# A memory stage with tokens on the partitions: numerators and denominators from one product, diagonals one item ahead

## What is computed

```python
def step(carry, inp):
    C, n, m = carry
    ...
    s = jnp.einsum('bthd,bshd->bhts', qc, kc) * jnp.exp(d - m_t[..., None])
    num = jnp.einsum('bhts,bshe->bhte', s, vc) + w_inter[..., None] * jnp.einsum('bthd,bhde->bhte', qc, C)
    den = s.sum(-1) + w_inter * jnp.einsum('bthd,bhd->bht', qc, n)
    h = num / jnp.maximum(jnp.abs(den), jnp.exp(-m_t))[..., None]
...
hn = hf * lax.rsqrt(jnp.mean(hf * hf, axis=-1, keepdims=True) + EPS)
hn = hn * g_ml.astype(jnp.float32).reshape(ML_HEADS, ML_V_DIM)
ml = hn.reshape(B, T, ML_WIDTH).astype(att.dtype) * jax.nn.sigmoid(o_pre)
```

## Time and profile before

| | us |
|---|---|
| time before, median of 3 runs | 2726.67 (2722.68 to 2727.57) |
| the profiled execution | 2733.2 |
| its span | 2731.4 |
| memory stage, layer 0: loop | 281.0 to 370.3 |
| first half of the output product, layer 0 | 370.3 to 389.3 |
| memory stage, layer 1: loop | 1030.8 to 1086.9 |
| first half of the output product, layer 1 | 1086.9 to 1096.6 |

### The profile page before, as it was taken

The page is one execution under the profiler, slowest core; times in us unless marked ns, Lnnn a source line. Parts: engine busy times, 40 slices in busy tenths (PEclk is TensorE's granted clock), DMA queues, the critical chain, the costliest instruction groups (busy, mean ns, idle before and its releaser), DMA issues.

```text
span 2731.4 us, 34159 instructions
## 1 busy us (share of the span) xinstructions
PE 2568.9 (94%) x13662; PEld 2099.3 (77%) x13662; DVE 1824.8 (67%) x2870; ACT 1310.2 (48%) x1937; POOL 29.5 (1%) x27
## 2 busy tenths in 40 slices
PE   6999998999999989799999999999989899998998
PEld 3464665778787658788888888887788899997998
DVE  4778433667532354399999989988867576576774
ACT  2135313222222243287777777776745454444543
POOL 0000000000000000000000000000000000000000
PEclk8999898999998998799999999999989999998999
DMA  6422001555421110298898888997933355432552
GB/s 280 186 101 100 1 31 62 192 207 185 160 102 62 47 47 1 93 356 328 334 357 328 332 339 329 349 334 301 366 133 111 125 182 191 151 139 100 178 182 97
DMA packets 71676, 512.08 MB, mean 187 GB/s; under 512 B 7904, under 2 KB 9056, under 8 KB 10048
## 3 DMA queue, kind: packets, MB, share of 16 engines
q1 hardware_dynamic: 68688, 500.20, 49.2%
q10 hardware_dynamic: 2208, 7.37, 0.7%
q0 software_dynamic: 592, 1.97, 0.2%
HBM read 507.27 MB, written 2.23 MB: 187 GB/s over the span
## 4 chain that ended last, share of the span: by engine, by line
PE 82%; DVE 9%; ACT 6%; issue 1%; DMA 1%; DVEq 0%; ACTq 0%
PE bank L767 81%; DVE UL L1906 2%; ACT UH L1456 1%; DVE arena L1906 1%; ACT arena L1459 1%; DVE arena L1914 1%; DVE HT L1906 1%; DMA XT<-in_x 1%; PE bank L1099 1%; ACT HT L1459 1%; DVE HGl L1906 1%; ACT XT L1459 0%; DVE arena L1910 0%; DVE JUNK L1953 0%; DVE small L1973 0%
## 5 line engine op out<-in xcount | busy, mean ns | idle before, releaser
L1906 DVE TENSOR_TENSOR UL<-ring,UH 128x1024 fp32r<-128x1024 f32 x738 | 886.1, 1212 | 216.1 <-ACT UH L1456 196.7
L1456 ACT CAST UH<-ring 128x1024 fp32r<-128x1024 f32 x738 | 761.2, 1039 | 353.6 <-PE bank L767 345.0
L767 PE MATMUL bank<-XH,UH 128*128 128x256 f32 x1040 | 308.2, 296 | 9.9 <-DVE XL L1906 8.8
L767 PE MATMUL bank<-UH,HGh 128*128 128x512 f32 (+1 forms) x768 | 293.1, 382 | 14.3 <-DVE HT L1906 10.3
L767 PE MATMUL bank<-XL,UH 128*128 128x256 f32 x1040 | 297.0, 286 | 0.0
L767 PE MATMUL bank<-XH,UL 128*128 128x256 f32 x1040 | 296.8, 285 | 0.0
L767 PE MATMUL bank<-UL,HGh 128*128 128x512 f32 (+1 forms) x768 | 289.1, 376 | 3.5 <-issue 3.5
L767 PE MATMUL bank<-UH,HGl 128*128 128x512 f32 (+1 forms) x768 | 289.7, 377 | 0.0
L1456 ACT CAST UH0a<-ring 128x1024 fp32r<-128x1024 f32 x66 | 69.0, 1048 | 319.9 <-PE bank L767 314.5
L767 PEld LDWEIGHTS bank<-XH,UH 128*128 128x128 f32 x1040 | 201.4, 194 | 22.4 <-issue 15.3
L1953 DVE CUSTOM_DVE_ANT_0 JUNK<-ring,CROW 128x1024 bf16<-128x1024 f32 x176 | 206.0, 1217 | 18.3 <-ACT CROW L1459 17.3
(11 more groups left out here) (206 smaller groups left out, 4513.5 us busy)
## 6 DMA issues: line engine op xcount, KB each, us to landing
ring<-in_w SPq DMA_DIRECT2D x477, 1024.0 KB, 4.8
XT<-in_x ACTq DMA_DIRECT2D x1, 2048.0 KB, 20.4
bias_scratch<-BIAS POOLq DMA_DIRECT2D x6, 192.0 KB, 2.1
consts<-in_c ACTq DMA_DIRECT2D x1, 1109.0 KB, 7.9
CROW<-in_r ACTq DMA_DIRECT2D x1, 1024.0 KB, 13.5
out_y<-XT ACTq DMA_DIRECT2D x2, 512.0 KB, 3.5
BIAS<-bias_scratch POOLq DMA_DIRECT2D x1, 768.0 KB, 5.7
constd<-in_c ACTq DMA_DIRECT2D x1, 768.0 KB, 4.1
```

The costliest lines, as they stand in the source:

```text
L767: return e.matmul(out, lhsT, rhs, start=start, stop=stop, skip_group_check=True)
L1456: return e.copy(out, in_)
L1906: return e.tensor_tensor(out, a, b, op)
```

## The change

`V_M` gets 129 columns a head, the last filled with ones by POOL (memories behind it move by 16 columns). The product of an item is turned: for each covered block of 128 target tokens the weighted scores are stationary and the 129 columns stream, so that a bank receives numerators with tokens on the partitions and, beside them, the denominators. A group takes two such banks in layer 0 (two blocks each), one in layer 1. The products with the column of ones, `feedback`, `divided`, `squares_of` and `norm_of` are gone. `denominator` reads the 129th columns; `first_of` on ACT multiplies the forward half by its reciprocals, which are now a scalar per partition, and `second_of` on DVE multiplies and adds the backward half. Squares are summed by ACT's accumulator. `scaled` applies the root by token, `turned` transposes back on TensorE (four blocks a head in layer 0, two in layer 1), and `gated` is one operation instead of two. On DVE the diagonal of item i is issued before the weighting of item i−1.

```diff
-        V_M = view(arena, 9728, 4, 512)
+        V_M = view(arena, 9728, 4, 4, 129)
-        NUM = view(HT, 0, 2, 4, 512)
+        NT = view(HT, 0, 4, 512)
...
+                def turned(h):
+
+                    b = take(w, ("turned", l, h))
+                    w.wait_ge(*vec.at("scaled1", l, h))
                     for t in tbs:
+                        op = e.transpose(b[:, 128 * t:128 * t + 128], NT[:, t, 128 * h:128 * h + 128], con("I"))
...
-                        for n_, (a, z) in enumerate(ranges(l, d, s)[2]):
-                            op = mm(psum(tile)[:, a:z], V_M[:, s, 128 * h:128 * h + 128], SWR1[:, j % 4, a:z],
-                                    j % 4 == 0 and n_ == 0, False)
-                            for t in range(a // 128, z // 128):
-                                op = mm(psum(den)[:, t:t + 1], SWR1[:, j % 4, 128 * t:128 * t + 128], con("one", 0, 1),
-                                        j % 4 == 0 and n_ == 0 and t == a // 128, False)
+                        blocks = [t for a, z in ranges(l, d, s)[2] for t in range(a // 128, z // 128)]
+                        for n_, t in enumerate(blocks):
+                            first = j % 4 == 0 and all(t_ // 2 != t // 2 for t_ in blocks[:n_])
+                            op = mm(psum(("num", l, g, t // 2))[:, 129 * (t % 2):129 * (t % 2) + 129],
+                                    SWR1[:, j % 4, 128 * t:128 * t + 128], V_M[:, s, h, :], first, False)
...
-                        if j % 4 == 1 and j > 4:
-                            feedback(g - 1)
-                        if j % 8 == 4 and j > 8:
-                            squares_of(j // 8 - 1)
...
+                    join_part(l, m, range(4))
+                    for h in ((0, 1), (2,), (), (3,))[m]:
+                        turned(h)
...
+                def first_of(h):
+
+                    g = 2 * h
+                    w.wait_ge(*vec.at("den", l, g))
+                    for t in range(2 * l, 4):
+                        tile = ("num", l, g, t // 2)
+                        apply(NT[:, t, 128 * h:128 * h + 128], psum(tile)[:, 129 * (t % 2):129 * (t % 2) + 128], ACT.Identity,
+                              scale=DEN[:, g, t:t + 1]).then_inc(*act.up(("first", l, h), free=[tile]))
...
+                    for t in range(2 * l, 4):
+                        e.activation(HS[:, h % 2, 128 * t:128 * t + 128], NT[:, t, 128 * h:128 * h + 128], ACT.Square, bias=0.0,
+                                     scale=1.0, accum_out=HRT[:, h, t:t + 1]).then_inc(*act.up(("hs", l, h)))
...
-                    if j % 4 == 0 and j:
-                        g = j // 4 - 1
-                        evict(("num", l, g), NUM[:, g % 2, g // 2, t0:512], psum(("num", l, g))[:, t0:512])
+                    if j % 8 == 5:
+                        first_of(j // 8)
...
+                def second_of(h):
+
+                    g = 2 * h + 1
+                    w.wait_ge(*act.at("first", l, h))
+                    w.wait_ge(*vec.at("den", l, g))
+                    for t in range(2 * l, 4):
+                        tile = ("num", l, g, t // 2)
+                        nt = NT[:, t, 128 * h:128 * h + 128]
+                        stt(nt, psum(tile)[:, 129 * (t % 2):129 * (t % 2) + 128], DEN[:, g, t:t + 1], nt, ALU.mult,
+                            ALU.add).then_inc(*vec.up(("both", l, h), free=[tile]))
...
-                for i in range(1, len(items) + 2):
+                for i in range(len(items) + 2):
...
+                            for k in range(i // 4 * 4, i):
+                                if ranges(l, *items[k][1:])[0]:
+                                    w.wait_ge(*act.at("far", l, k))
+                            if i >= 2:
+                                w.wait_ge(*vec.at("sw", l, i - 2))
+                            stt(WT[:, i % 2, dg:dg + 128], psum(("nb", l, i // 4))[:, dg:dg + 128], ucol,
...
+                    if 1 <= i < len(items) + 1:
+                        j = i - 1
```

More of the change, by code:

```diff
@@ new lines, in gated @@
+                def gated(h):
+                    tile = ("turned", l, h)
+                    w.wait_ge(*sums.at(*tile))
+                    w.wait_ge(*act.at("sig", l, h))
+                    stt(H[:, 4 + h, t0:512], psum(tile)[:, t0:512], par(f"gml{l}", h), OM[:, h, t0:512], ALU.mult,
+                        ALU.mult).then_inc(*vec.up(("cat", l, h), free=[tile]))
+                for i in range(len(items) + 2):
+                    if i < len(items):
+                        h, d, s = items[i]
+                        dg = ranges(l, d, s)[1]
@@ L2141, in memory @@
                             w.wait_ge(*sums.at("mv", l, j - 4))
-                        for a, z in cover:
+                        for a, z in ranges(l, *items[j][1:])[2]:
                             stt(SWR1[:, j % 4, a:z], psum(("ms", l, j))[:, a:z], 0.125, WT[:, j % 2, a:z], ALU.mult,
```

159 lines of the change are left out of this document (58 added, 101 removed).

## The result

| | before | changed |
|---|---|---|
| median | 2726.12 us (4 runs, 2722.68 to 2727.57) | 2673.68 us (4 runs, 2673.01 to 2676.05) |
| ratio, 95% interval | | 0.9813 [0.9801, 0.9825] |
| profiled execution, its span | 2733.2, 2731.4 us | 2673.33, 2671.5 us |

A forecast was written before the change was run, and what follows sets the result against it. TensorE was taken as the bound, with DVE and ACT more than half free. Savings of 29.6 and 16.8 us in the loops, 2.4 and 1.0 at the ends, sum to 49.8, for a median of 2676.9 us, range 2661 to 2698.

The forecast's parts named there:

- Part 1: One product for numerator and denominator: 0.243 us a block, saving 13.8 us in layer 0 and 9.6 in layer 1.
- rival of unhidden loads: In the block products, weight loads are not hidden: 0.60 us a block, 49 us more, 2726; chance 0.02.
- Part 2: No feedback, squares to ACT; with Part 1, TensorE's layer 0 head takes 11.1 us instead of 17.3, layer 1's 7.3.
- Part 3: Work of DVE and ACT per head of layer 0: 10.4 and 8.4 us, against TensorE's 11.1.
- Part 4: In the loops, diagonal i+1 issued before weighting i: a 0.9 us cycle hidden behind TensorE's 1.4 us item.
- Where they meet: Layer 0, at a head's two denominators: waits of 0.65 and 0.2 us, slips of 0.3 each; a group 6.3.
- The first group: Layer 0's first group, with the chain to the first item and moments: 11.0 us, before 18.2; upper bound 15.
- The ends: After the loops, first half of the output product: 16.6 us against 19.0 in layer 0, 8.7 against 9.7 in layer 1.
- Hand-overs bind: In the loops, DVE's work and its waits for ACT stand end to end: 14.4 us a head, 2689; chance 0.17.
- TensorE alone: In the loops, no waits, slips or clock loss: 5.54 and 3.65 us a group, 2665; chance 0.12.
- clock rival: TensorE at its lower clock (1.2 GHz) throughout both stages: 32 us more, 2759; chance 0.03.
- return of the gain through the experts' weights: Layer 1's gain is given back to the weight traffic of the experts: 2695; chance 0.03.

The follow-up runs named there:

- a2_ones_back: The changed kernel with an extra one-column product on the same weights beside each of the 136 block products, numbers unused; 2689.7 us, 0.9881.
- a1_diag_same: The changed kernel with DVE's old order, the diagonal of item j directly before the weighting of item j; 2688.8 us, 0.9861.
- c1_wide_moments: The changed kernel with the moments of the attention output streaming 128 columns of ones instead of one; 2668.8 us, 0.9802.
- a4_dve_load: The changed kernel with one more DVE operation of 128 columns before each of the 64 weightings; 2679.4 us, 0.9840.
- a3_wide_back: The changed kernel with an extra product of 128 columns of ones beside each of the 136 block products; 2686.6 us, 0.9864.
- c4_filler: The changed kernel with moments streaming 128 columns and, in layer 1's 7.35 us wait for ACT, 16 products on constants; 2663.9 us, 0.9776.
- b2_wide_ones: The kernel before with its denominator products streaming 128 columns of ones instead of one; 2722.0 us, 0.9981.
- b1_ahead_only: The kernel before with only DVE's diagonals one item ahead and ACT signalling the far exponential by itself; 2714.2 us, 0.9964.
- b3_few_ones: The kernel before without 88 of its 136 one-column denominator products; 2714.6 us, 0.9960.

## Why the prediction was right, and where it was off

- **What bounds.** TensorE with idle neighbours: right. The forecast left the bound with TensorE and expected small waits at the denominators; so it came.
- **Part 1.** 0.243 a block predicted, 0.236 measured with the load. The rival of unhidden loads (0.60 a block) is out. So is, here, the rule weighed there (the Trainium skill, TensorE: Matmul & The Clock Gate, The mechanism), as far as it names other row groups only: full-height loads stand beside full-height products at 0.118 us a record. The same section also lets a load be pulled ahead when it goes to the background weight buffer, which the prediction left out and which this trace does not contradict. A one-column product came at 0.22 us rather than 0.20 (a2_ones_back), so the two forms differ less than the prediction had it.
- **Part 2.** TensorE's head of 11.1 us: two groups have 5.51 and 5.83 us of records, 11.3. Right.
- **Part 3.** DVE's and ACT's prices were high by a fifth: a head has 8.4 us of DVE and 6.9 us of ACT (304.05 to 315.67), where 10.4 and 8.4 were predicted. The sign "DVE busy near 80%" did not come; it is 65%. The denominator with the norm's scalars was to take 0.95 + 0.35 and takes 0.88; without them 0.60 (321.46 to 322.07); `second_of` 1.1 where 1.4 was priced, `first_of` 1.14 for 1.3, the four squares with their reads 1.3 for 1.6:

```profile
300.10 0.31 ACT L1550 ACTIVATE arena<-HT 128x128 f32<-128x128 f32 x1 [0.87 <-DVE HT L1900]
300.32 0.19 ACT L1550 ACTIVATION_READ_ACCUMULATOR arena<-HT 128x1 f32 x1
300.41 0.29 ACT L1550 ACTIVATE arena<-HT 128x128 f32<-128x128 f32 x1
...
304.78 1.14 ACT L1436 ACTIVATE HT<-bank,tokens 128x128 f32<-128x128 f32 x4 [0.77 <-DVE tokens L2078]
...
311.16 1.11 DVE L1900 SCALAR_TENSOR_TENSOR HT<-bank,tokens,HT 128x128 f32<-128x128 f32 x4
```

- **Part 4.** Right for the changed kernel (a1_diag_same: 13 to 18 us). Not foreseen: its worth to the kernel before.
- **Where they meet.** This term was mis-sized. A steady group was to be 6.3 us and is 5.8. The walk gave a wait of 0.65 us at the first meeting because the denominator was priced 0.4 too long; 0.20 to 0.28 us came. The "slips of 0.3 each" at the second bank and the square, added without a row, did not come at all, nor did the 0.2 of the second meeting. In layer 1 two errors cancel: groups of 3.91 and 4.16 us, 8.07 a head against 8.15, with 7.56 us of records for the 7.3 predicted and 0.51 us of waits for 0.9:

```profile
1009.35:1013.51 4.16, 3.77 (x25) 3.38 (x24) 2.69 (x11) 2.23 (x7) 0.00 (x0) 1.00 0.00 0
1013.51:1017.42 3.91, 3.79 (x25) 3.38 (x24) 2.89 (x12) 2.29 (x9) 0.00 (x0) 1.00 0.00 0
```

- **The first group.** 11.0 predicted, 12.9 measured, inside the bound of 15. The size of the clock's share was wrong. Before, 10.2 of the 18.2 us stood at the lower level (0.72). Without it and without 1.8 us of products the group would have been 11.3, so my 11.0 left nothing of it. It shrank to 3.4 of 12.9 us (0.87) and cost 1.7; it stands behind the moments, which the change keeps. c1_wide_moments has the 11.3.
- **Clock behind the first group.** 2 us predicted, none came: every group from the second shows 1.00.
- **The last group** has no scores of following items: 3.7 us (327.13 to 330.83), where I counted 6.3. A plain omission.
- **The ends.** The four transposes of a head take 0.44 us from start to start (338.57 to 339.01 in the changed kernel), where I had taken the duration of a row, 0.63, against my own rule that the step is the price. The wait of 0.4 us did not come either.
- **Sum.** Layer 0: first group +1.9, second 0, third 6.4 for 7.8 (−1.4; the `att_norm` operations cost 0.6 there, not 1.5), four middle groups −2.1, the last −2.6, clock −2.0: −6.2, 53.6 for 59.7. Layer 1: 38.4 for 39.3. Ends 15.5 for 16.6 and 8.1 for 8.7.
- **Whole.** The four stretches gave 58.5 us in the profiled executions, forecast 49.8; the medians gave 52.4. The 6 us between lie mostly with the kernel before: its profiled execution was 7 us above its median, at a mean clock of 0.953 over the program. Its 39 executions beside the experiments fit that: the four at 0.952 or 0.953 took 2732.3 to 2736.7 us, the 27 at 0.955 or more 2719.1 to 2728.5. So two errors partly cancelled. The changed kernel's stretches were forecast 8.8 us too long (124.3 for 115.5), and the saving was counted from a long execution. That the median came within 3.2 us of 2676.9 is in part luck.
- **Rivals.** "Hand-overs bind" did not happen, yet by a4_dve_load 0.38 of any further work on DVE would be exposed. "TensorE alone" (2665, 5.54 us a group) was nearest for the steady groups of layer 0. Neither the clock rival nor the return of the gain through the experts' weights showed: outside the stretches the two kernels' executions spend 2557.4 and 2556.0 us.

## What to carry to other kernels

A product that streams one column costs nearly as much as one of 128; a sum over the contraction belongs into the product that already has these weights loaded, as one more column. Moving results so that the scalar they need lies on the partition removes not only a product but the round trip behind it: here order and hand-overs, with the clock that came with them, were 15 to 19 of 58.5 us by the stretches and 22 of 51 by the ratios, which a count of TensorE's records would not show. And when a group is summed up, walk the first and the last one by themselves; both were where this prediction missed most.

## What the runs showed of the hardware

- An fp32 product takes 0.22 us beside others, load included, whether it streams 1, 128 or 129 columns (a2_ones_back 0.44 us for two, a3_wide_back 0.45; rows of one form 0.218 and 0.236).
- In layer 0's loop the 32 one-column records of the moments have a stretch at the clock's lower level (0.50, which is 1.2 GHz) that begins within or right behind them in eleven of twelve profiles. In the changed kernel TensorE was busy without a gap from 280 to 290 us, and the level fell at 285.2. With 128 columns in their place and equal time the clock stays at 1.00 (c1_wide_moments, c4_filler). It also stays at 1.00 with the one-column moments in a3_wide_back, whose other products around them are all wide.
- The same exchange in the denominators of the kernel before goes with a clock of 0.96 for 0.89 in that loop and 5 us less time (b2_wide_ones), with extra products 0.95 became 1.00 (a2_ones_back to a3_wide_back). But 0.96 also came with the diagonals ahead and all one-column products in place (b1_ahead_only). A wide product with unused columns can be the faster one.
- Fewer records can go with a lower clock: b3_few_ones, 0.84 for 0.89, with 4.8 us more of waits.
- Activity in a wait need not keep the clock: after 4.0 us of filler and 3.4 us of waiting the next 5.1 us ran at 0.50.
